# All expert sums on TensorE's four column strips, in a kernel whose gathers bring four slots of 32 tokens

## The reference, cut to what matters

```python
def block(xb):                                   # 128 tokens
    q = (xb @ w_q).reshape(PEER_BLOCK, PEER_HEADS, 2, PEER_QDIM // 2)
    s = jnp.einsum('thpd,hpnd->thpn', q, sub_keys)
    s1, i1 = lax.top_k(s[:, :, 0], 16)
    s2, i2 = lax.top_k(s[:, :, 1], 16)
    cand = (s1[..., :, None] + s2[..., None, :]).reshape(128, 8, 256)
    ...
    e_idx = jnp.take_along_axis(cand_idx, pos, axis=-1)
    gate = jax.nn.softmax(top_s, axis=-1)
    act = gelu(einsum('thkd,td->thk', u[e_idx], xb))
    return einsum('thk,thkd->td', gate * act, v[e_idx])
```

## Time and profile before

| | us |
|---|---|
| median of 3 runs | 4593.66 |
| lowest and highest | 4587.42, 4599.04 |
| profiled execution, its span | 4603.1 |
| TensorE busy | 3506.8 (76%) |
| VectorE busy | 3006.1 (65%) |
| ScalarE busy | 1562.3 (34%) |
| POOL busy | 1422.6 (31%) |
| DMA, gathers | 1073.81 MB, 59.7% of 16 engines |
| DMA, weights | 237.98 MB, 14.5% |
| mean granted TensorE clock | 0.879 |

### The profile page before, as it was taken

The page is one execution under the profiler, slowest core; times in us unless marked ns, Lnnn a source line. Parts: engine busy times, 40 slices in busy tenths (PEclk is TensorE's granted clock), DMA queues, the critical chain, the costliest instruction groups (busy, mean ns, idle before and its releaser), DMA issues.

```text
span 4603.1 us, 46492 instructions
## 1 busy us (share of the span) xinstructions
PE 3506.8 (76%) x13760; PEld 2275.4 (49%) x13760; DVE 3006.1 (65%) x6158; ACT 1562.3 (34%) x4216; POOL 1422.6 (31%) x1140
## 2 busy tenths in 40 slices
PE   7898966778887786877879785787878785577676
PEld 4676753446565643435657552345646562222222
DVE  2322248768778758848778748768768747965544
ACT  2223124442343233442243333443252333333333
POOL 0110002344311232334422223235321223356574
PEclk8899988888888897997889897898889888899899
DMA  7213347776876889995688877796687678899997
GB/s 252 83 39 103 110 158 299 303 272 255 316 269 225 355 330 355 354 386 210 229 326 358 334 291 301 291 379 229 235 335 282 271 281 329 324 397 417 406 414 322
DMA packets 247803, 1314.74 MB, mean 286 GB/s; under 512 B 21248, under 2 KB 35456, under 8 KB 116480
## 3 DMA queue, kind: packets, MB, share of 16 engines
q0 software_dynamic: 147456, 1073.81, 59.7%
q1 hardware_dynamic: 100096, 237.98, 14.5%
HBM read 1309.61 MB, written 2.10 MB: 285 GB/s over the span
## 4 chain that ended last, share of the span: by engine, by line
DVE 27%; PE 25%; DMA 12%; issue 9%; ACT 7%; DVEq 7%; POOL 5%; PEld 5%; ACTq 2%; PEldq 1%; SPq 0%; POOLq 0%
DVE row L1514 9%; DMA row<-uv,e_idx 9%; PE bank L625 6%; POOL row L1900 5%; PE bank L686 4%; DVE e_acc L1484 4%; PE bank L793 3%; PE bank L1004 3%; DMA weights<-w_ada 2%; DVEq L1480 2%; DVE reg L1402 2%; PEld bank L672 2%; PE bank L784 2%; PEld bank L686 1%; DVEq L1822 1%
## 5 line engine op out<-in xcount | busy, mean ns | idle before, releaser
L1900 POOL DMA_INDIRECT row<-uv,e_idx x1024 | 1269.8, 1240 | 2877.2 <-DVE e_acc L1484 1103.9
L1514 DVE CUSTOM_DVE_ANT_0 row<-row,e_h 128x1024 f32<-128x1024 f32 x1024 | 1297.9, 1277 | 619.4 <-DMA row<-uv,e_idx 562.2
L625 PE MATMUL bank<-row,e_diag 128*128 128x512 f32 x2440 | 1249.5, 647 | 440.1 <-ACT e_diag L1080 378.4
L625 PEld LDWEIGHTS bank<-row,e_diag 128*128 128x128 f32 x2440 | 459.3, 202 | 1112.6 <-ACT e_diag L1080 569.1
L1073 ACT ACTIVATE e_ge<-e_dot 128x1 f32<-128x1 f32 x1024 | 207.2, 202 | 1864.6 <-DVE e_dot L1514 1846.2
L1484 DVE SCALAR_TENSOR_TENSOR e_acc<-row,e_wg,e_acc 128x1024 f32<-128x1024 f32 x406 | 526.4, 1296 | 58.8 <-ACTq L1077 19.9
L686 PE MATMUL bank<-hT,weights 128*128 128x256 f32 (+2 forms) x2176 | 518.9, 395 | 42.9 <-ACT hT L1142 24.8
L686 PEld LDWEIGHTS bank<-hT,weights 128*128 128x128 f32 (+2 forms) x2176 | 416.5, 193 | 164.0 <-issue 50.7
L672 PE MATMUL bank<-hT,weights 128*128 128x256 f32 x1536 | 355.9, 385 | 26.1 <-issue 22.4
L672 PEld LDWEIGHTS bank<-hT,weights 128*128 128x128 f32 x1536 | 285.1, 191 | 95.9 <-issue 55.9
L1075 ACT ACTIVATE e_wg<-e_gate,e_ge 128x1 f32<-128x1 f32 x1024 | 301.5, 294 | 73.5 <-issue 1.7
(11 more groups left out here) (252 smaller groups left out, 3546.7 us busy)
## 6 DMA issues: line engine op xcount, KB each, us to landing
weights<-w_ada SPq DMA_DIRECT2D x48, 1024.0 KB, 8.4
weights<-w_mac SPq DMA_DIRECT2D x64, 768.0 KB, 6.0
weights<-w_in SPq DMA_DIRECT2D x44, 1024.0 KB, 7.9
weights<-w_mb SPq DMA_DIRECT2D x32, 768.0 KB, 7.6
weights<-w_out SPq DMA_DIRECT2D x16, 1024.0 KB, 12.9
weights<-w_pq SPq DMA_DIRECT2D x16, 1024.0 KB, 9.9
row<-uv,e_idx POOLq DMA_INDIRECT x1024, 8.5
weights<-w_in SPq DMA_DIRECT2D x8, 1056.0 KB, 5.5
```

What stands on the lines that cost most here:

```text
L625: last = mm(acc_ps[k][:, :], e_diag[:, r, :], row[r][:, D + k * NB:D + (k + 1) * NB], start=(e, j) in PE_FIRST, stop=(e, j) in PE_LAST)
L1514: V.tensor_tensor_reduce(row[r][:, 0:D], row[r][:, 0:D], e_h[t][:], 1.0, 0.0, ALU.mult, ALU.add, e_dot[:, r:r + 1]).then_inc(dots, 1)
L1900: pool.indirect_dma_start(row[r], None, uv, bass.IndirectOffsetOnAxis(ap=e_idx[:, j:j + 1], axis=0)).then_inc(rows_landed[r], 16)
```

## The change

A gather no longer brings one slot of 128 tokens but four slots of 32 tokens. A unit is 32 tokens (`QT`) with 32 gathers (`USLOTS`), a lap has 8 units (`UNITS`) and as many gathers as before, 256 with the same bytes. Partition 32 q + p of a gather belongs to token p of the unit. So:

- the routing rearranges its indices and gates, with 16 small copies between quarters of the partitions and two copies into place;
- `e_rep` holds the 32 tokens' rows four times, once for each quarter. TensorE spreads them (ident columns as weights, on four strips, a bank for each half of the columns) and ScalarE copies them out; two such buffers alternate;
- `e_diag` is 128x32: ident's four quarters added to a mask, times the weight. The matmul with it sums the four slots of a token at once;
- all slots are added by TensorE, VectorE adds none. Two gathers are added together, at the second of a pair: each gather has two halves of 512 columns, so there are four matmuls of 128x32, one for each strip of output partitions of one bank. `acc_ps` alternates between units;
- at the end of a unit ScalarE copies the bank to `e_sum`, TensorE multiplies its 128-column blocks with `sel`, which adds the two strips of a half and transposes, and VectorE multiplies with the modulation and adds to `xT`, in two operations;
- ScalarE's gelu is made for a pair; POOL's gather waits for the pair that held its row;
- `PACE`, `LAG` of TensorE (3.5 to 2.2) and the places of the routing pieces are new. The two scans over the decay masks become 8 and 8 shorter scans without masks, and the two masks are no longer loaded.

```diff
-PACE = dict(head=(8, 6), prep=(74, 76), scan=(47, 47), gla=(22, 22), dsa=(8, 9), mac=(24, 18), att=(4, 6), mb=(21, 21), out=(8, 8),
-            pq=(12, 14), route=(30, 31))
+PACE = dict(head=(8, 6), prep=(62, 62), scan=(60, 60), gla=(22, 22), dsa=(12, 12), mac=(28, 26), att=(6, 10), mb=(18, 18), out=(8, 8),
+            pq=(10, 10), route=(26, 26))
...
-LAG = dict(POOL=-2.5, DVE=0.5, ACT=0.8, PE=3.5)
-N_SLOT = 2 * SLOTS
+LAG = dict(POOL=-2.5, DVE=0.5, ACT=0.8, PE=2.2)
+N_SLOT = UNITS * USLOTS
+EVICT_AT, TURN_AT, WRITE_AT = 2, 2, 5
+SPREAD_AT, SPREAD_COPY_AT = (6, 10), (9, 13)
+PIECES, SOFT_AT = {}, {}
+for _th, _at, _soft in (((0, 1), (0, 1, 3, 4, 6, 7, 9, 10), 9), ((1, 0), range(16, 40, 3), 33), ((1, 1), range(40, 64, 3), 57)):
...
         def _(pe):
+            def spread(g, x, b):
+                t, lo = g % UNITS // 4, QT * (g % 4)
+                for c in range(4):
+                    last = mm(acc_ps[b][c * QT:(c + 1) * QT, :], ident[:, lo:lo + QT], e_h[t][:, x * NB:(x + 1) * NB], start=True, stop=True)
+                last.then_inc(spread_filled, 1)
+
+            def turn_unit(g):
+                pe.wait_ge(unit_copied, g + 1)
+                for k in range(KD):
+                    dh, i = k // 4, k % 4
+                    last = mm(acc_ps[g % 2][:, k * QT:(k + 1) * QT], e_sum[:, i * P:(i + 1) * P], sel[:, dh * QT:(dh + 1) * QT],
+                              start=True, stop=True)
+                last.then_inc(unit_turned, 1)
...
-                    if not on_dve(e, j):
-                        pe.wait_ge(diag_ready, PE_COUNT[n])
-                        for k in range(2):
-                            last = mm(acc_ps[k][:, :], e_diag[:, r, :], row[r][:, D + k * NB:D + (k + 1) * NB],
-                                      start=(e, j) in PE_FIRST, stop=(e, j) in PE_LAST)
-                        last.then_inc(pe_rows, 1)
+                    if s % 2:
+                        pe.wait_ge(diag_ready, n // 2 + 1)
+                        for x in range(2):
+                            r = (n - 1 + x) % RING
+                            for dh in range(2):
+                                c = 2 * x + dh
+                                last = mm(acc_ps[g % 2][c * QT:(c + 1) * QT, :], e_diag[:, r, :], row[r][:, D + dh * NB:D + (dh + 1) * NB],
+                                          start=(s == 1), stop=(s == USLOTS - 1))
+                        last.then_inc(pairs_summed, 1)
...
         def _(act):
+                    if s % 2:
+                        act.wait_ge(dots, n + 1)
+                        A(e_ge[:, r - 1:r + 1], e_dot[:, r - 1:r + 1], ACT.Gelu)
                         act.drain()
+                        for x in range(2):
+                            A(e_wg[:, r - 1 + x:r + x], e_gate[:, j - 1 + x:j + x], ACT.Copy, scale=e_ge[:, r - 1 + x:r + x])
+                        act.drain()
+                        for x in range(2):
+                            last = A(e_diag[:, r - 1 + x, :], mask, ACT.Copy, scale=e_wg[:, r - 1 + x:r + x])
+                        last.then_inc(diag_ready, 1)
...
+                    for q in range(4):
+                        for g in range(4):
+                            V.tensor_copy(e_post[QT * g:QT * (g + 1), :, q, :], e_pre[QT * q:QT * (q + 1), :, ET * g:ET * (g + 1)])
+                    dve.drain()
+                    V.tensor_copy(places_in(e_idx), e_post[:, 0])
+                    V.tensor_copy(places_in(e_gate), e_post[:, 1])
...
-                    if s:
-                        weighted(j - 1)
...
                     if n >= RING:
-                        e0, j0 = (n - RING) // N_SLOT, (n - RING) % N_SLOT
-                        if j0 % SLOTS == SLOTS - 1:
-                            pool.wait_ge(turned, 2 * (TH * e0 + j0 // SLOTS + 1))
-                        elif on_dve(e0, j0):
-                            pool.wait_ge(dve_rows, DVE_COUNT[n - RING])
-                        else:
-                            pool.wait_ge(pe_rows, PE_COUNT[n - RING])
-                    pool.wait_ge(routed, 4 * e + 2 * t + s // 64 + 1)
+                        pool.wait_ge(pairs_summed, (n - RING) // 2 + 1)
+                    pool.wait_ge(routed, 4 * e + 2 * t + s % USLOTS // ET + 1)
```

More of the change, by code:

```diff
@@ L35 @@
 QUADS = 2 * TH
+QT = P // 4
+USLOTS = SLOTS // 4
+UNITS = 4 * TH
 COLS = {}
@@ L633, in turn_tile @@
-            def turn_tile(e, t):
-                pe.wait_ge(combined, TH * e + t + 1)
-                summed = row[(e * N_SLOT + (t + 1) * SLOTS - 1) % RING]
-                for k in range(2):
-                    for i in range(4):
-                        last = nc.tensor.transpose(acc_ps[k][:, i * P:(i + 1) * P], summed[:, k * NB + i * P:k * NB + (i + 1) * P], ident)
-                    last.then_inc(turned, 1)
-            pe.wait_ge(loaded, 16 * 7)
+            def spread(g, x, b):
[3 more added lines that the diff above has]
+                last.then_inc(spread_filled, 1)
@@ L1470, in expert_steps @@
                 modc_e, h0 = modc_all[:, 48 * (e // 2):48 * (e // 2) + 48], TH * (e % 2)
-                def weighted(j):
-                    if not on_dve(e, j):
-                        return
-                    n = e * N_SLOT + j
-                    r = n % RING
-                    v, w = row[r][:, D:2 * D], e_wg[:, r:r + 1]
-                    dve.wait_ge(wg_ready, DVE_COUNT[n])
-                    dve.drain()
-                    if j % SLOTS == 0:
-                        V.tensor_scalar(e_acc[:], v, w, None, ALU.mult).then_inc(dve_rows, 1)
-                    else:
-                        V.scalar_tensor_tensor(out=e_acc[:], in0=v, scalar=w, in1=e_acc[:], op0=ALU.mult, op1=ALU.add).then_inc(dve_rows, 1)
@@ L1502, in expert_steps, with write_x @@
-                for j in range(N_SLOT):
-                    n = e * N_SLOT + j
-                    r, t, s = n % RING, j // SLOTS, j % SLOTS
-                    for t_, hh, i in PIECES.get(j, ()):
+                def write_x(g):
+                    dve.wait_ge(unit_turned, g + 1)
+                    u = g % UNITS
+                    xs = xT[:, :, h0 * P + u * QT:h0 * P + (u + 1) * QT]
+                    y = v3(acc_ps[g % 2][:, 0:KD * QT], KD)
+                    V.tensor_tensor(y, y, bc(modc_e[:, 40:48].unsqueeze(2), [P, KD, QT]), ALU.mult)
+                    dve.drain()
+                    V.tensor_tensor(xs, y, xs, ALU.add)
+                    dve.drain().then_inc(unit_out, 1)
@@ L1506, in expert_steps @@
+                for j in range(N_SLOT):
+                    u, s = j // USLOTS, j % USLOTS
+                    g, n = UNITS * e + u, e * N_SLOT + j
+                    r = n % RING
+                    if j in PIECES:
+                        t_, hh, i = PIECES[j]
                         piece(i, e, t_, hh)
-                    if t and s == 0:
-                        dve.drain()
-                        weighted(j - 1)
-                        combine(0)
                     if s == 0:
-                        dve.wait_ge(*G["h2_copied"].at(e, 2 * (t + 1)))
+                        dve.wait_ge(spread_copied, 2 * g + 2)
@@ L1513, in expert_steps @@
                     dve.wait_ge(rows_landed[r], 16 * (n // RING + 1))
-                    V.tensor_tensor_reduce(row[r][:, 0:D], row[r][:, 0:D], e_h[t][:], 1.0, 0.0, ALU.mult, ALU.add, e_dot[:, r:r + 1]).then_inc(dots, 1)
-                    if s:
-                        weighted(j - 1)
-                    if t and s == WRITE_AT:
-                        write_x(0)
+                    V.tensor_tensor_reduce(row[r][:, 0:D], row[r][:, 0:D], e_rep[g % 2], 1.0, 0.0, ALU.mult, ALU.add, e_dot[:, r:r + 1]).then_inc(dots, 1)
@@ L1519, in expert_steps @@
+                    if u and s == WRITE_AT:
+                        write_x(g - 1)
                     yield True
-                dve.drain()
-                weighted(N_SLOT - 1)
-                combine(1)
-                write_x(1)
+                write_x(UNITS * e + UNITS - 1)
             for i, e in enumerate((EPS, LN_EPS, KK_EPS, 1.0)):
@@ L1613, in _ @@
                         for c_ in range(4):
-                            V.tensor_tensor_scan(r_cs[:, c_, :], m128, r_sg[:, c_, :], 0.0, ALU.mult, ALU.add)
+                            for t_ in range(TH):
+                                ts = slice(t_ * P, (t_ + 1) * P)
+                                V.tensor_tensor_scan(r_cs[:, c_, ts], ones, r_sg[:, c_, ts], 0.0, ALU.mult, ALU.add)
                         for c_ in range(4):
@@ L1735, in _ @@
                 for c in range(2):
-                    V.tensor_tensor_scan(g_cum[:, c, :], m64, g_la[:, c, :], 0.0, ALU.mult, ALU.add)
+                    for n in range(NCH):
+                        ns = slice(n * CH, (n + 1) * CH)
+                        V.tensor_tensor_scan(g_cum[:, c, ns], ones[:, 0:CH], g_la[:, c, ns], 0.0, ALU.mult, ALU.add)
                 dve.drain()
```

160 lines of the change are left out of this document (76 added, 84 removed).

## The result

The changed kernel took 4493.22 us (median of 4 runs, 4485.1 to 4500.17), the kernel before 4592.07 in the same comparison: ratio 0.9784, interval 0.977 to 0.9799. It is 99 us faster where 292 were forecast, and 3 us above the stated range. The profiled execution took 4485.1 us, its span 4483.3.

The account below looks back on a forecast made before the run. Laps were taken as dense on TensorE, VectorE and DMA, which wait for each other; the tail as DMA-full. 189 us less inserted work a lap gave 292 us off the 4603 span: 4311, so 4300 us, range 4080 to 4490.

Parts of the forecast that it names:

- Part 1, the strips: Expert matmuls on TensorE: four strips run together, a pair takes 1.28 us (bounds 0.91 and 1.89), 164 us a lap against 218.
- The sum: Laps: inserted work falls from 851 to 662 us; at shares 0.58 and 0.46, 308 us less, 292 after routing at lap ends.
- VectorE's 181 us: VectorE's weighted adds in the laps: 164 us plus 17 us idle before them, 127 wait-and-add steps, leave VectorE each lap.
- 4.4 us a unit: TensorE work per 32-token unit: a spread of 2 x 1.28 us and a turn of 1.8 us, +35 us a lap.
- The tail: Last lap's slots running alone: DMA stays full, rows held 6.5 and 5.2 us; change 0, between -5 and +40 us.
- The clock fell: Rival: lighter TensorE work takes the laps' granted clock from 0.86 to 0.75, costing 140 us, total 4440; chance 0.07.
- Gathers as the bound: Rival: time saved turns into VectorE's waits for rows, 60% of the gain goes, total 4480; chance 0.08.
- TensorE waiting for VectorE: Rival: pairs queued before trunk matmuls wait for dots and diagonals; if one in three does, 435 us, total 4740; chance 0.08.
- Routing and small parts: Each routing unit gains sixteen small copies, two more and three drains: 4 us, bounds 2 and 6; scans and masks under 1 us.
- The tail's first 64 slots: Start of the tail, counted as VectorE work: 190 us before, 194 us after.

Follow-up runs that it names:

- pace_before: The changed kernel with the old `PACE` of the kernel before (more slots in the preparation, fewer in the scan): 4618.04 us.
- b_no_adds: The kernel before with VectorE's weighted adds left out of the sum, waits and drains kept: 4447.94 us.
- pairs_twice: The changed kernel with the four matmuls of each pair issued twice in the three laps, not in the tail: 4634.31 us.
- ring8_lag14: The changed kernel with eight row buffers in the tail and TensorE 1.4 slots behind the plan in the laps instead of 2.2: 4540.16 us.

## Why the prediction was wrong

- **Part 1, the strips: right, and a little too dear.** They run together. A pair between trunk matmuls takes 0.99 us from its start to the next one's at full clock, not 1.28. That is the median of the 320 pairs in the laps that had other work right behind them; one in seven took 1.9 us, at the half clock. One of them:

```profile
3044.83 1.06 PE L634 MATMUL bank<-row,e_diag 128*32 128x512 f32 x8
3045.82 1.16 PE L783 MATMUL bank<-reg 128*128 128x128 f32 x8
```

  The drain that the Trainium skill (TensorEngine Tiling (Array Packing), Key Properties) puts on each change of mode is at most 0.99 - 0.86 = 0.13 us here, with 0.86 for two records one after the other, against 0.30 in the earlier trace rows.
- **The sum: the step that failed.** The prediction turned 189 us a lap of inserted work into 308 us of time; pace_before, the same change with slots where they had stood, brought 37. "How much of inserted work lengthens a lap comes from the laps themselves" gave one factor, 0.46 to 0.58, and applied it to VectorE's 181 us wherever they stood. Of those adds 423 us in 503 stood in the middle, where TensorE was next in line and was given their work. Taken out without giving it to anyone they were worth 0.29, in the middle 0.26 (b_no_adds). What TensorE is given there costs 0.6 (pairs_twice). An estimate for the three middles of pace_before, with these two prices: 423 us of VectorE less are 110 us gained; TensorE had 44 slots of 1.72 us there, 76 us, and now has 187 pairs of 0.99 and, by the prediction's own 4.4 us a unit, some 12 units, 238 us in all; 162 more are 97 us lost. 13 us remain, 30 were measured. And TensorE's relief fell mostly on the head, where doubling its pairs costs 4 to 12 us a lap. With 37 us for the strips alone, the rest of the 169 is the new `PACE` on top of them, which the prediction left out of the sum.
- **The tail: failed too.** "8.7 us of flight stay, over three gathers, so DMA stays full" had the hold wrong. On the mean of both rows of a pair it was 7.6 us (7.95 in the first of the pair shown), where 6.5 and 5.2 had been counted. The flight was indeed 8.7 us, but at 2.73 us a slot and 382 GB/s, so DMA did not stay full. In the pair shown the second dot began 2.5 us after the first, so that gelu started after 3.75 us, where two dots in a row had been counted with 2.6; ScalarE took 1.4, TensorE 1.9, and POOL's start 0.9, which the sum left out. It cost 45 us, 5 over the bound given.
- **Rivals.** The clock fell, to 0.83 and 0.84 in the laps (head 0.70) and 0.52 in the tail. In the tail it did matter, against the text, by way of the row's hold. Gathers as the bound: landing rows went up on the chain, and half their bytes would give 120 us in the laps, so that rival named a part of it, not its cause. TensorE waiting for VectorE happened, 418 us, over the 300 that I had set as a mark for wrong. 392 of them stood in heads and ends, and what they cost there is only known in part: TensorE had room in the heads (pairs_twice). In the middle such waits cost, as ring8_lag14 showed, but at a lag of 2.2 there were only 26 us of them.
- **Routing and small parts.** The copies are L1494, 256 of 179 ns, 46 us in all; the estimate of 4 us a unit stands. The tail's first 64 slots took 196 us, 194 were forecast, and that was luck: the forecast counted VectorE's work as their bound, but with eight buffers the same work took 175.

What stays open: why the middle costs about 0.6 of the TensorE time added to it rather than all, and what besides VectorE sets the pace of the head at 3.7 us a slot; halving the dots moved it by under 20 us and halving the gathers by 7, 23 and 6. No run filled TensorE in the heads, so what their clock of 0.70 costs is not known either, nor what the pairing costs in the laps.

## What to carry to other kernels

A factor from the mean of a loop holds only for work that stands evenly in it: cut the loop by stages, write down which engine is full in each, and price a moved piece where it lands, at the engine that takes it. A faster engine is worth something only together with a new distribution of the work; here each alone brought 0 to 37 us and both 169. And when batching makes a consumer faster, count how long it keeps its input buffers: at a full DMA the ring must cover hold plus flight. Here two buffers that lay idle brought 67 us in the tail, where the change had lost 45.

## What was not expected of the hardware

- TensorE's granted clock in the tail fell from 0.92 to 0.52 when its busy time there fell from 470 to 300 us; with filling it was 0.99 in the last 192 slots, with single slots, 329 us busy of 482, 0.67.
- Gathers of 1 MB came at 416 GB/s with eight buffers and at 382 with six and a longer hold, though the DMA engines counted as busy 0.97 of the time: a share near one is not yet a full rate. The GB/s beside it tell.
